# Attention on stacked high and low parts: two score products over 128 rows for three over 64, two value products for three

## The chip, the cores and the metric

One core of one Trainium2 chip runs the whole program. The metric is the device time of one execution in microseconds (us); lower is better. TensorE is called PE in the views, and its weight loads PEld; VectorE is DVE, ScalarE is ACT, GpSimd is POOL, and SyncE, which issues most of the DMAs, is SP.

## The reference, cut to what matters

The model has two layers on 1024 tokens of width 1024. Layer 0 is a gMLP mixer and an FFN; layer 1 is chunked band attention and an FFN. The change touches the attention only.

```python
def chunk_attention(h, w_qkv, rel_bias, w_out):      # SEQ 1024, 16 heads of 64, CHUNK 64
    ...
    def one_chunk(c):
        ...
        s = jnp.einsum('bqhd,bkhd->bhqk', qc, kc).astype(jnp.float32) * scale + bias
        ...
        p = jax.nn.softmax(s, axis=-1).astype(vc.dtype)
        return jnp.einsum('bhqk,bkhd->bqhd', p, vc)
    ...
    return o @ w_out
```

Each chunk of 64 queries sees its own chunk and the 8 chunks before it. Everything is float32.

## The kernel before, in words

**Split numbers.** TensorE multiplies in a shortened float32 (`F32R`). To keep the precision, each operand is held as a high part and a low part (the rest), and a product is three matmuls into one PSUM tile: high with high, high with low, low with high. The helper `product` issues them from lines 434, 435 and 436, so these three lines carry nearly all of TensorE's work, whatever the stage.

**Pairs of heads.** The attention walks over 8 pairs of heads. Pair 0 and pair 7 are written out, pairs 1 to 6 are one loop body. For each pair the projections q, k and v are made from the normed input (`part`, 8 products of 512 columns for each half of the tokens), and q of the next pair is made within this one. A pair of heads fills 128 partitions: head 0 is rows 0 to 63, head 1 rows 64 to 127.

**Steps and passes.** A pair has 16 steps s (8 blocks of 128 queries, two heads each). `step(s)` gives block i and head; the order of the blocks and heads is 0, 1 for head 0, then 0, 1 for head 1, then 2, 3, and so on. From step 8 on the window of keys is full, 640 columns (`WIN`); before that it is 128 to 512. The program has 19 passes m, in which the engines' work is laid out by hand as a pipeline:

- `scores_of(m)` on TensorE writes the scores into PSUM, DVE adds the bias and takes the row maximum (the custom instruction on L1142) and negates it (L1146), ACT takes the exponential (L856).
- For step m-1, DVE inverts the row sum (`rowinv`, L1128) and ACT scales the probabilities (L851).
- For step m-2, `transpose_probs` turns them on TensorE (L597) into `probs_t`, ACT copies the high part out (`pt_hi`, L846) and DVE makes the low part (`pt_lo`, L1132).
- In every second pass from 4 on, `values(c)` multiplies the turned probabilities of block pair c with `vz_hi` and `vz_lo` into bank 3. In `vz_*` the columns of the other head are zero, so that both heads add up in one 128-row tile of outputs: head 0 lands on partitions 0 to 63 and head 1 on 64 to 127.
- In passes 10 and 18, bank 3 holds the outputs of 512 queries; ACT copies the high part (`o_hi`, L867) and DVE the low part (`o_lo`, L1161), and `out_product` multiplies them with the output weights, one tile of 8 per slot (`out0` in passes 11 to 18, `out1p` in passes 3 to 7 of the next pair). DVE adds each to `x` (L1098).
- In pass 14, ACT and DVE take the next pair's q out of its bank (L825 and L1086).

Each engine runs its own instructions strictly in the written order, and the engines meet at semaphores. There is one `scores` tile and one `probs_t` tile: scores of pass m wait for the bias instruction of pass m-1, transposes of step s wait for the scaled probabilities of s and for `pt_lo` of s-1.

**Other engines.** POOL splits every weight unit into its two parts (L352, L354) from `raw`, which SP fills by DMA.

Of the kernel before, what the change touches and what calls it, by code (L numbers as in the profile page):

```python
# [82 lines left out]
def trunk(nc, x_t, gains, v_gain, w_s_t, b_s, rel_rev, ident_d, w_units, out_t):  # L83
# [4 lines left out]
    with ExitStack() as ctx:  # L88
# [65 lines left out]
        pt_lo += [sb("pt_lo1", [P, 2 * WIN // P, P], F32R)]  # L154
        o_hi = sb("o_hi", [P, HALF], F32R)
# [44 lines left out]
        bias_in, bias_masked, vz_zero = sem("bias_in"), sem("bias_masked"), sem("vz_zero")  # L200
# [98 lines left out]
        def in_heads(vz, h, view=lambda ap: ap):  # L299

            return view(vz[:, 4 * h:4 * h + 4, :, :]).rearrange("p t a (b c) -> p t (a b) c", c=HD)[:, :, 0::3, :]
# [128 lines left out]
        def _(pe):  # L430
# [147 lines left out]
            def scores_of(it, s):  # L578
                i, head = step(s)
                rows = slice(head * HD, (head + 1) * HD)  # L580
# [19 lines left out]
            def values(it, c):  # L600
# [5 lines left out]
                if c % 4 == 0:  # L606
                    ge(pe, o_lo_done, it * 2 + i // 4)

                both = [(key, 0, 2) for key in range(max(0, i - LEFT + 1), i + 1)]
                for key, q, n in both + ([(i - LEFT, 0, 1)] if i >= LEFT else []) + [(i + 1, 1, 1)]:  # L610
                    tiles = WIN // P
                    at = q * tiles + key - (i + q - LEFT)
                    cols = slice((i % 4 + q) * P, (i % 4 + q + n) * P)
                    out = bank[3][:, cols]
                    if n == 2:
# [82 lines left out]
        def _(act):  # L698
# [129 lines left out]
            def attention(it, first, last):  # L828
                def query_hi(it, h, name="q"):
                    p_hi_part(it, name, h, flipped(q_hi[:, toks(h)]), tiled(p_bank(it, name, h)[:, :]), HD ** -0.5)  # L830

                if first:
                    load_bias(0)
                    query_hi(-1, 0)
                    p_hi_part(it, "k", 0, k_hi[:, toks(0)])
                    hi_tiles(2, 1)
                    query_hi(0, 1, "q first")
                else:
                    p_hi_part(it, "k", 0, k_hi[:, toks(0)])
                p_hi_part(it, "k", 1, k_hi[:, toks(1)])  # L840
                for m in range(19):
# [17 lines left out]
                    if m in (1, 3):  # L859
                        p_hi_part(it, "vt", m // 2, in_heads(vz_hi, m // 2), by_head(p_bank(it, "vt", m // 2)))  # L860
# [43 lines left out]
        def _(dve):  # L904
# [179 lines left out]
            def query_lo(it, h, name="q", number=None):  # L1084
                dve.wait_ge(p_hi, it * 6 + (2 + 5 + h) if number is None else number)
                dve.scalar_tensor_tensor(flipped(q_lo[:, toks(h)]), tiled(p_bank(it, name, h)[:, :]), HD ** -0.5,  # L1086
                                         flipped(r32(q_hi[:, toks(h)])), ALU.mult, ALU.subtract).then_inc(p_read, 1)
# [7 lines left out]
            def attention(it, first, last):  # L1095
# [9 lines left out]
                def keys_lo(h, number):  # L1105
                    p_lo_part(it, "k", h, number, k_lo[:, toks(h)], r32(k_hi[:, toks(h)]))

                if first:
# [6 lines left out]
                    for part in (vz_hi, vz_lo):  # L1115
                        for head in range(2):
# [160 lines left out]
```

## Time and profile before

| what | us |
|---|---|
| median of 3 runs | 2829.72 |
| the three runs | 2825.27, 2831.75, 2829.72 |
| span of the profiled execution | 2829.8 |
| PE busy | 2715.2 (96%) |
| PEld busy | 2229.6 (79%) |
| DVE busy | 1244.1 (44%) |
| ACT busy | 594.2 (21%) |
| POOL busy | 798.9 (28%) |

The span runs from the first to the last instruction of one profiled execution; the page shows no time of its own around it, and the span lies 0.1 us from the median of the runs. The busy times are averages over stages that are limited by different things, so the attention is read by itself. It lies between about 1400 and 2074 us. A matmul's shown duration overlaps the next one's; what one costs in a dense row of them is the distance between their starts.

### The profile page before, as it was taken

What the parts mean: (1) busy time and instruction counts of PE and PEld (TensorE: products, weight loads), DVE (VectorE), ACT (ScalarE), POOL (GpSimd) and SP (SyncE); (2) the same over time, 40 slices, a digit from 0 to 9 for tenths busy, and PEclk for the clock granted to TensorE, in tenths of its full rate; (3) what the DMA queues carried; (4) which work ended last, traced back from release to release, by engine and by line L of the source; (5) the groups of instructions that cost most, each with busy time, mean ns of one, the idle gap of its engine ahead of it and who ended that gap; (6) DMA issues with size and microseconds to landing.
All of it is one profiled execution on the core that took longest, in us unless ns stands there. A gap on an engine that the chain in (4) does not pass through costs nothing.

```text
span 2829.8 us, 34050 instructions
## 1 busy us (share of the span) xinstructions
PE 2715.2 (96%) x12660; PEld 2229.6 (79%) x12660; DVE 1244.1 (44%) x1998; ACT 594.2 (21%) x1091; POOL 798.9 (28%) x450
## 2 busy tenths in 40 slices
PE   6999999998999999999899999999979999999997
PEld 5877877776888888888678888888758888888885
DVE  7215555567333322222754444455583233332225
ACT  3111111123000000000354433444430000000002
POOL 3232223223333333333211101111113333333334
PEclk9999999999999999999989999999999999999998
DMA  4222121111111111111100101110001111111101
GB/s 136 101 94 78 54 70 61 46 54 52 53 52 44 44 52 52 44 44 45 39 32 31 39 17 39 39 39 31 30 23 52 52 52 52 44 44 52 52 30 60
DMA packets 53220, 143.50 MB, mean 51 GB/s; under 512 B 5392, under 2 KB 15776, under 8 KB 53168
## 3 DMA queue, kind: packets, MB, share of 16 engines
q1 hardware_dynamic: 35632, 119.71, 12.8%
q10 hardware_dynamic: 17536, 23.07, 2.4%
q8 instruction: 35, 0.57, 0.1%
q14 instruction: 17, 0.14, 0.0%
HBM read 130.13 MB, written 12.63 MB: 50 GB/s over the span
## 4 chain that ended last, share of the span: by engine, by line
PE 45%; DVE 3%; issue 1%; ACT 1%; DVEq 0%; ACTq 0%
PE bank L434 11%; PE bank L436 10%; PE bank L435 10%; PE scores L434 3%; PE scores L435 2%; PE scores L436 2%; PE probs_t L597 2%; PE probs_t L436 1%; PE probs_t L435 1%; PE probs_t L434 1%; DVE full L927 0%; DVE prob L1142 0%; DVE rstd L917 0%; PE bank L648 0%; DVE acc L909 0%
## 5 line engine op out<-in xcount | busy, mean ns | idle before, releaser
L434 PE MATMUL bank<-hn_hi,w_hi 128*128 128x512 f32 x2048 | 818.3, 400 | 26.5 <-DVE hn_lo L932 22.1
L436 PE MATMUL bank<-hn_hi,w_lo 128*128 128x512 f32 x2048 | 805.3, 393 | 0.0
L435 PE MATMUL bank<-hn_lo,w_hi 128*128 128x512 f32 x2048 | 805.0, 393 | 0.0
L352 POOL TENSOR_SCALAR w_hi<-raw 128x1024 fp32r<-128x1024 f32 x212 | 248.1, 1170 | 1967.0 <-PE bank L436 1392.1
L354 POOL TENSOR_TENSOR w_lo<-raw,w_hi 128x1024 fp32r<-128x1024 f32 x212 | 518.2, 2444 | 17.7
L434 PEld LDWEIGHTS bank<-hn_hi,w_hi 128*128 128x128 f32 x2048 | 389.0, 190 | 119.1 <-DVE hn_lo L932 17.6
L436 PEld LDWEIGHTS bank<-hn_hi,w_lo 128*128 128x128 f32 x2048 | 389.0, 190 | 83.3
L435 PEld LDWEIGHTS bank<-hn_lo,w_hi 128*128 128x128 f32 x2048 | 389.5, 190 | 78.9 <-issue 1.2
L1002 DVE TENSOR_TENSOR full<-bank,atmp 128x512 f32<-128x512 f32 x88 | 60.9, 692 | 715.9 <-ACT atmp L806 714.3
L806 ACT ACTIVATE atmp<-bank 128x512 f32<-128x512 f32 x88 | 52.6, 598 | 1152.6 <-PE bank L436 1152.5
L1011 DVE TENSOR_TENSOR x<-probs_t,x 128x512 f32<-128x512 f32 x240 | 162.7, 686 | 110.6 <-PE probs_t L436 110.3
L1011 DVE TENSOR_TENSOR x<-scores,x 128x512 f32<-128x512 f32 x240 | 162.5, 687 | 95.6 <-PE scores L436 92.7
L1004 DVE TENSOR_TENSOR h_lo<-full,h_hi 128x512 fp32r<-128x512 f32 x88 | 128.5, 1460 | 61.5 <-ACT h_hi L767 61.5
L434 PE MATMUL scores<-h_hi,w_hi 128*128 128x512 f32 x352 | 137.5, 391 | 2.2 <-DVE h_lo L1004 1.6
L435 PE MATMUL scores<-h_lo,w_hi 128*128 128x512 f32 x352 | 137.3, 390 | 0.0
L436 PE MATMUL probs_t<-h_hi,w_lo 128*128 128x512 f32 x352 | 137.1, 390 | 0.0
L434 PE MATMUL probs_t<-h_hi,w_hi 128*128 128x512 f32 x352 | 136.9, 389 | 0.0
L435 PE MATMUL probs_t<-h_lo,w_hi 128*128 128x512 f32 x352 | 136.9, 389 | 0.0
L436 PE MATMUL scores<-h_hi,w_lo 128*128 128x512 f32 x352 | 136.9, 389 | 0.0
L856 ACT ACTIVATE prob<-prob,negmax 128x640 f32<-128x640 f32 (+4 forms) x128 | 89.2, 697 | 154.4 <-DVE negmax L1146 154.4
L1132 DVE TENSOR_TENSOR pt_lo<-probs_t,pt_hi 128x640 fp32r<-128x640 f32 (+4 forms) x128 | 83.7, 654 | 65.1 <-ACT pt_hi L846 63.6
L1098 DVE TENSOR_TENSOR x<-bank,x 128x512 f32<-128x512 f32 x128 | 86.1, 687 | 38.0 <-PE bank L436 37.2
(141 smaller groups left out, 3757.5 us busy)
## 6 DMA issues: line engine op xcount, KB each, us to landing
raw<-w_units_in SPq DMA_DIRECT2D x212, 512.0 KB, 3.3
v_raw<-v_scratch ACTq DMA_DIRECT2D x16, 512.0 KB, 4.4
bias<-rel_scratch ACTq DMA_DIRECT2D x8, 640.0 KB, 3.8
x<-x_t_in SPq DMA_DIRECT2D x16, 256.0 KB, 6.5
v_scratch<-atmp ACTq DMA_DIRECT2D x16, 256.0 KB, 2.5
v_scratch<-full ACTq DMA_DIRECT2D x16, 256.0 KB, 2.6
out_t<-x SPq DMA_DIRECT2D x16, 256.0 KB, 2.0
ws_raw<-w_s_t_in ACTq DMA_DIRECT2D x8, 64.0 KB, 4.0
```

What stands on the lines that cost most here:

```text
L352: pool.tensor_scalar(w_hi[slot][:, :], raw[r][:, :], 1.0, 1.0, ALU.mult, ALU.mult).then_inc(w_split, 1)
L354: pool.tensor_tensor(w_lo[slot][:, :], raw[r][:, :], r32(w_hi[slot][:, :]), ALU.subtract).then_inc(w_split, 1)
L434: pe.matmul(out, lh, rh, start=start, stop=False)
L435: pe.matmul(out, lh, rl, start=False, stop=False)
L436: last = pe.matmul(out, ll, rh, start=False, stop=stop)
L597: t = pe.transpose(probs_t[:, j * P:(j + 1) * P], prob[s % 2][:, j * P:(j + 1) * P], ident[:, :])
L856: act.activation(prob[m % 2][:, off:], prob[m % 2][:, off:], ACT.Exp, bias=negmax[:, m % 2:m % 2 + 1], accum_out=rowsum[:, m % 2:m % 2 + 1 ...
L1002: dve.tensor_tensor(full[f][:, :], up, in1, ALU.mult).then_inc(s.full, 1)
L1004: dve.tensor_tensor(lo[:, f, toks(h)], full[f][:, :], r32(hi_part[:, f, toks(h)]), ALU.subtract).then_inc(s.lo, 1)
L1011: dve.tensor_tensor(x[:, n, toks(h)], bank[4 + d % 4][:, :], x[:, n, toks(h)], ALU.add).then_inc(s.added, 1)
L1098: dve.tensor_tensor(x[:, n, toks(h)], p_bank(it, name, n)[:, :], x[:, n, toks(h)], ALU.add).then_inc(p_read, 1)
L1132: dve.tensor_tensor(pt_tiles(pt_lo, s), tiled(probs_t[:, window(s):WIN]), r32(pt_tiles(pt_hi, s)), ALU.subtract).then_inc(pt_lo_done, 1)
```

## The change

The query tile `q2` holds, for head 0, the high part on rows 0 to 63 and the low part on rows 64 to 127 (for head 1 the other way round). `k2_hi` holds the keys' high part on both halves of the rows, and `k2_lo` holds the low part on the head's own rows and zeros on the others. One matmul over 128 rows with `k2_hi` gives high-high plus low-high; one with `k2_lo` gives high-low. For the values, `v2` holds the high part in the head's own 64 columns and the low part in the other 64, in place of zeros. Two matmuls (with `pt_hi` and `pt_lo`) give the high parts' result on the head's own partitions and the low parts' result on the other 64. These two halves have to be added afterwards: each head has its own half of bank 3 now (256 queries at a time), ACT copies the side part across (`o_move`), and DVE adds it (`o_add`) into `o_full` in SBUF, from which `o_hi` and `o_lo` are made. The zeros of the `vz` tiles (4 memsets) go, those of `k2_lo` (2 memsets) come, and the first scores wait for them.

```diff
-        q_hi = sb("q_hi", [P, SEQ], F32R)
-        q_lo = sb("q_lo", [P, SEQ], F32R)
-        k_hi = sb("k_hi", [P, SEQ], F32R)
-        k_lo = sb("k_lo", [P, SEQ], F32R)
-        vz_hi = sb("vz_hi", [P, BLOCKS, 2, P], F32R)
-        vz_lo = sb("vz_lo", [P, BLOCKS, 2, P], F32R)
+        q2 = sb("q2", [P, 2, SEQ], F32R)
+        k2_hi = sb("k2_hi", [P, 2, SEQ], F32R)
+        k2_lo = sb("k2_lo", [P, 2, SEQ], F32R)
+        v2 = sb("v2", [P, BLOCKS, 2, P], F32R)
...
+        o_side = sb("o_side", [P, 2 * P])
+        o_full = sb("o_full", [P, HALF])
...
             def scores_of(it, s):
...
                 if s == 0:
                     pe.wait_ge(p_read, p_number(it, "k", 1) + 1)
+                    pe.wait_ge(k2_zero, 2)
...
-                    product(scores[:, SHIFT + at:SHIFT + to], (q_hi[rows, tq], q_lo[rows, tq]), (k_hi[rows, tk], k_lo[rows, tk]),
-                            True, True, qk_done if to == WIN else None)
+                    out = scores[:, SHIFT + at:SHIFT + to]
+                    pe.matmul(out, q2[:, head, tq], k2_hi[:, head, tk], start=True, stop=False)
+                    mm = pe.matmul(out, q2[:, head, tq], k2_lo[:, head, tk], start=False, stop=True)
+                mm.then_inc(qk_done, 1)
...
             def values(it, c):
...
-                if c % 4 == 0:
-                    ge(pe, o_lo_done, it * 2 + i // 4)
+                if c % 2 == 0:
+                    ge(pe, o_added, it * 8 + c)
...
-                    product(out, (vz_hi[:, key, head, :], vz_lo[:, key, head, :]), parts,
-                            head == 0 and key == both[0][0] and n == 2, head == 1 and q == 1,
-                            pv_done if q == 1 else None)
+                    pe.matmul(out, v2[:, key, head, :], parts[0], start=head == 0 and key == both[0][0] and n == 2, stop=False)
+                    mm = pe.matmul(out, v2[:, key, head, :], parts[1], start=False, stop=head == 1 and q == 1)
...
+                def key_hi(h):
+                    act.wait_ge(p_done, p_number(it, "k", h) + 1)
+                    for to in range(2):
+                        for head in range(2):
+                            op = act.activation(k2_hi[rows_of(head if to == 0 else 1 - head), head, toks(h)],
+                                                p_bank(it, "k", h)[rows_of(head), :], ACT.Copy)
+                    op.then_inc(p_hi, 1)
+
+                def o_move(tiles):
+                    act.wait_ge(pv_done, it * 8 + (2 * tiles + 2))
+                    ge(act, o_added, it * 8 + 2 * tiles)
+                    for head in range(2):
+                        act.activation(o_side[rows_of(head), :], bank[3][rows_of(1 - head), head * 2 * P:(head + 1) * 2 * P],
+                                       ACT.Copy).then_inc(o_moved, 1)
...
+                    if m in (6, 10, 14, 18):
+                        o_move((m - 6) // 4)
                     if m in (10, 18):
-                        act.wait_ge(pv_done, it * 8 + (4 if m == 10 else 8))
+                        act.wait_ge(o_added, it * 8 + (4 if m == 10 else 8))
...
-                        act.activation(flipped(o_hi[:, :]), tiled(bank[3][:, :]), ACT.Copy).then_inc(o_hi_done, 1)
+                        act.activation(flipped(o_hi[:, :]), tiled(o_full[:, :]), ACT.Copy).then_inc(o_hi_done, 1)
...
+                def o_add(tiles):
+                    ge(dve, o_hi_done, it * 2 + tiles // 2)
+                    dve.wait_ge(o_moved, it * 8 + (2 * tiles + 2))
+                    for head in range(2):
+                        rows = rows_of(head)
+                        dve.tensor_tensor(o_full[rows, tiles % 2 * 2 * P:(tiles % 2 + 1) * 2 * P],
+                                          bank[3][rows, head * 2 * P:(head + 1) * 2 * P], o_side[rows, :],
+                                          ALU.add).then_inc(o_added, 1)
...
                     if m == 14 and not last:
                         query_lo(it, 0)
...
+                    if m in (6, 10, 14, 18):
+                        o_add((m - 6) // 4)
```

The high part of q is now written in two instructions of 64 rows in place of one of 128, that of k in four; their low parts are made in two each. `key_hi` and `o_move` run on ACT, `o_add` on DVE.

How the instructions stand on ACT in pass 10 of a middle pair, before and then after the change; `o_side` is the tile that `o_move` fills, `pt_hi` the turned probabilities' high part:

```order
L856 ACTIVATE prob,rowsum<-prob,negmax 128x640
L864 REGISTER_ALU
L866 REGISTER_ALU
L867 ACTIVATE o_hi<-bank 128x4x128
L846 ACTIVATE pt_hi<-probs_t 128x640
```

```order
L885 ACTIVATE prob,rowsum<-prob,negmax 128x640
L855 REGISTER_ALU
L858 ACTIVATE o_side<-bank 64x256 x2
L897 REGISTER_ALU
L898 ACTIVATE o_hi<-o_full 128x4x128
L875 ACTIVATE pt_hi<-probs_t 128x640
```

Two copies stand ahead of `o_hi`, `o_hi` reads what DVE adds up in between, and the next step's `pt_hi` stands behind all of it.

The same for DVE in pass 14 of a middle pair, from the negated maximum of that pass to the low part of the next pass, before and then after:

```order
L1146 TENSOR_SCALAR negmax<-rowmax 128x1
L1085 REGISTER_ALU
L1086 SCALAR_TENSOR_TENSOR q_lo<-bank,q_hi 128x4x128
L1097 REGISTER_ALU
L1098 TENSOR_TENSOR x<-bank,x 128x512
L1128 RECIPROCAL rowinv<-rowsum 128x1
L1132 TENSOR_TENSOR pt_lo<-probs_t,pt_hi 128x640
```

```order
L1193 TENSOR_SCALAR negmax<-rowmax 128x1
L1116 REGISTER_ALU
L1118 SCALAR_TENSOR_TENSOR q<-bank,q 64x4x128 x2
L1149 REGISTER_ALU
L1152 TENSOR_TENSOR o_full<-bank,o_side 64x256 x2
L1131 REGISTER_ALU
L1132 TENSOR_TENSOR x<-bank,x 128x512
L1175 RECIPROCAL rowinv<-rowsum 128x1
L1179 TENSOR_TENSOR pt_lo<-probs_t,pt_hi 128x640
```

One instruction has become two, two more have come in between, and `rowinv` stands behind them.

## Rows read from the trace of the kernel before

**Rows 1.** The page's first line.

```profile
span 2829.8 us, 34050 instructions
```

**Rows 2.** Busy time by stretch, one pair of heads (start:end, us, busy us, clock, DMA).

```profile
1572.00:1654.00 82.00, 81.36 (x453) 67.32 (x452) 41.31 (x108) 35.41 (x73) 13.73 (x8) 1.00 0.10 34
```

**Rows 3.** PE's timeline, one pair: start, duration (us), line, operation.

```profile
1671.48 0.32 PE L434 MATMUL scores<-k_hi,q_hi 64*128 64x128 f32 x1
...
1700.92 0.71 PE L597 MATMUL probs_t<-ident,prob 128*128 128x128 f32 x5
1701.56 0.44 PE L434 MATMUL scores<-k_hi,q_hi 64*128 64x384 f32 x1
...
1702.19 0.28 PE L434 MATMUL scores<-k_hi,q_hi 64*128 64x256 f32 x1
1702.31 0.28 PE L435 MATMUL scores<-k_lo,q_hi 64*128 64x256 f32 x1
...
1702.63 0.39 PE L434 MATMUL bank<-pt_hi,vz_hi 128*128 128x256 f32 x1
...
1708.01 0.71 PE L597 MATMUL probs_t<-ident,prob 128*128 128x128 f32 x5
...
1721.80 0.71 PE L597 MATMUL probs_t<-ident,prob 128*128 128x128 f32 x5
...
1724.32 0.71 PE L597 MATMUL probs_t<-ident,prob 128*128 128x128 f32 x5
...
1728.32 0.71 PE L597 MATMUL probs_t<-ident,prob 128*128 128x128 f32 x5
```

**Rows 4.** Groups of instructions on PE in the attention, shapes apart.

```profile
L436 PE MATMUL bank<-pt_hi,vz_lo 128*128 128x256 f32 x192 | 54.4, 283 | 0.0
...
L436 PE MATMUL scores<-k_hi,q_lo 64*128 64x256 f32 x128 | 36.2, 283 | 0.0
...
L436 PE MATMUL scores<-k_hi,q_lo 64*128 64x384 f32 x64 | 21.5, 336 | 0.0
```

**Rows 5.** Timeline of ACT and DVE in pass 14 of the same pair.

```profile
1717.32 0.71 ACT L846 ACTIVATE pt_hi<-probs_t 128x640 fp32r<-128x640 f32 x1 [0.53 <-PE probs_t L597]
...
1718.06 0.83 DVE L1132 TENSOR_TENSOR pt_lo<-probs_t,pt_hi 128x640 fp32r<-128x640 f32 x1 [0.60 <-ACT pt_hi L846]
...
1718.80 0.81 DVE L1142 CUSTOM_DVE_ANT_0 prob<-scores,bias 128x640 f32<-128x640 f32 x1
...
1719.85 0.83 ACT L856 ACTIVATE prob<-prob,negmax 128x640 f32<-128x640 f32 x1 [1.11 <-DVE negmax L1146]
...
1720.67 0.57 ACT L825 ACTIVATE q_hi<-bank 128x512 fp32r<-128x512 f32 x1
...
1721.28 0.69 DVE L1086 SCALAR_TENSOR_TENSOR q_lo<-bank,q_hi 128x512 fp32r<-128x512 f32 x1 [1.47 <-ACT q_hi L825]
...
1722.61 0.15 DVE L1128 RECIPROCAL rowinv<-rowsum 128x1 f32<-128x1 f32 x1
```

**Rows 6.** Timeline in pass 10: the outputs' high and low parts.

```profile
1705.09 0.58 ACT L867 ACTIVATE o_hi<-bank 128x512 fp32r<-128x512 f32 x1
...
1705.70 0.69 DVE L1161 TENSOR_TENSOR o_lo<-bank,o_hi 128x512 fp32r<-128x512 f32 x1 [1.47 <-ACT o_hi L867]
```

**Rows 7.** Timeline: instructions of 256 columns on ACT and DVE.

```profile
1686.60 0.36 ACT L846 ACTIVATE pt_hi<-probs_t 128x256 fp32r<-128x256 f32 x1
...
1686.99 0.42 DVE L1132 TENSOR_TENSOR pt_lo<-probs_t,pt_hi 128x256 fp32r<-128x256 f32 x1
```

**Rows 8.** Timeline at the start of pair 0, PE and then DVE.

```profile
1421.99 0.32 PE L434 MATMUL scores<-k_hi,q_hi 64*128 64x128 f32 x1 [1.41 <-DVE k_lo L1082]
...
1421.99 1.02 DVE L1117 MEMSET vz_hi<- 128x512 f32 x2
```

**Rows 9.** Busy time by stretch behind pair 7: PE first, the granted clock third from the end.

```profile
2066.58:2069.99 3.41, 0.00 (x0) 0.00 (x0) 3.37 (x4) 0.34 (x1) 0.00 (x0) 1.00 0.00 0
2069.99:2073.41 3.42, 3.14 (x7) 2.29 (x8) 3.42 (x7) 0.96 (x3) 0.00 (x0) 0.50 0.00 0
```

More of the change, by code:

```diff
@@ L297, in tiled, with rows_of, v2_part @@
             return ap.rearrange("p (t c) -> p t c", c=P)
-        def in_heads(vz, h, view=lambda ap: ap):
-            return view(vz[:, 4 * h:4 * h + 4, :, :]).rearrange("p t a (b c) -> p t (a b) c", c=HD)[:, :, 0::3, :]
+        def rows_of(head):
+            return slice(head * HD, (head + 1) * HD)
+        def v2_part(h, lo):
+            quarters = v2[:, 4 * h:4 * h + 4, :, :].rearrange("p t a (b c) -> p t (a b) c", c=HD)
+            return quarters[:, :, 1:3, :] if lo else quarters[:, :, 0::3, :]
         def by_head(ap):
@@ L829, in query_hi @@
                 def query_hi(it, h, name="q"):
-                    p_hi_part(it, name, h, flipped(q_hi[:, toks(h)]), tiled(p_bank(it, name, h)[:, :]), HD ** -0.5)
+                    act.wait_ge(p_done, p_number(it, name, h) + 1)
+                    for head in range(2):
+                        op = act.activation(flipped(q2[rows_of(head), head, toks(h)]),
+                                            tiled(p_bank(it, name, h)[rows_of(head), :]), ACT.Copy, scale=HD ** -0.5)
+                    op.then_inc(p_hi, 1)
[5 more added lines that the diff above has]
+                                                p_bank(it, "k", h)[rows_of(head), :], ACT.Copy)
+                    op.then_inc(p_hi, 1)
+                def o_move(tiles):
[4 more added lines that the diff above has]
+                                       ACT.Copy).then_inc(o_moved, 1)
                 if first:
@@ L838, in attention @@
                 else:
[L839 to L840 removed]
+                    key_hi(0)
+                key_hi(1)
                 for m in range(19):
@@ L1085, in query_lo @@
                 dve.wait_ge(p_hi, it * 6 + (2 + 5 + h) if number is None else number)
-                dve.scalar_tensor_tensor(flipped(q_lo[:, toks(h)]), tiled(p_bank(it, name, h)[:, :]), HD ** -0.5,
-                                         flipped(r32(q_hi[:, toks(h)])), ALU.mult, ALU.subtract).then_inc(p_read, 1)
+                for head in range(2):
+                    op = dve.scalar_tensor_tensor(flipped(q2[rows_of(1 - head), head, toks(h)]),
+                                                  tiled(p_bank(it, name, h)[rows_of(head), :]), HD ** -0.5,
+                                                  flipped(r32(q2[rows_of(head), head, toks(h)])), ALU.mult, ALU.subtract)
+                op.then_inc(p_read, 1)
             def mask_bias(it):
@@ L1105, in keys_lo @@
                 def keys_lo(h, number):
-                    p_lo_part(it, "k", h, number, k_lo[:, toks(h)], r32(k_hi[:, toks(h)]))
+                    dve.wait_ge(p_hi, it * 6 + (2 + number))
+                    for head in range(2):
+                        rows = rows_of(head)
+                        op = dve.tensor_tensor(k2_lo[rows, head, toks(h)], p_bank(it, "k", h)[rows, :],
+                                               r32(k2_hi[rows, head, toks(h)]), ALU.subtract)
+                    op.then_inc(p_read, 1)
+                def o_add(tiles):
+                    ge(dve, o_hi_done, it * 2 + tiles // 2)
+                    dve.wait_ge(o_moved, it * 8 + (2 * tiles + 2))
+                    for head in range(2):
+                        rows = rows_of(head)
+                        dve.tensor_tensor(o_full[rows, tiles % 2 * 2 * P:(tiles % 2 + 1) * 2 * P],
+                                          bank[3][rows, head * 2 * P:(head + 1) * 2 * P], o_side[rows, :],
+                                          ALU.add).then_inc(o_added, 1)
                 if first:
@@ L1114, in attention @@
                     keys_lo(1, 2)
-                    for part in (vz_hi, vz_lo):
-                        for head in range(2):
-                            dve.memset(r32(part[:, :, head, (1 - head) * HD:(2 - head) * HD]), 0.0).then_inc(vz_zero, 1)
+                    for head in range(2):
+                        dve.memset(r32(k2_lo[rows_of(1 - head), head, :]), 0.0).then_inc(k2_zero, 1)
                     mask_bias(0)
@@ L1158, in attention @@
                         out_add("out1p", 1, n)
+                    if m in (6, 10, 14, 18):
+                        o_add((m - 6) // 4)
                     if m in (10, 18):
                         dve.wait_ge(o_hi_done, it * 2 + (1 if m == 10 else 2))
-                        dve.tensor_tensor(flipped(o_lo[:, :]), tiled(bank[3][:, :]), flipped(r32(o_hi[:, :])),
+                        dve.tensor_tensor(flipped(o_lo[:, :]), tiled(o_full[:, :]), flipped(r32(o_hi[:, :])),
                                           ALU.subtract).then_inc(o_lo_done, 1)
```

16 lines of the change are left out of this document (9 added, 7 removed).

## The prediction

> **What bounds the kernel now.** The page gives the span [rows 1]; nothing is shown around it, and it lies 0.1 us above the median of the runs, so I sum against 2829.8. The change lives in the attention only, so the next view is the busy time of one pair of heads: in 82 us TensorE (PE) is busy for 81.4, VectorE (DVE) for 41.3 and ScalarE (ACT) for 35.4 [rows 2]. That reads like a pair bound by TensorE, from which every matmul taken away is time won. The timelines are read next, to see how far behind TensorE the softmax loop of ACT and DVE is, since a busy share can't show that. The reader should see a loop with a period of its own, little below what TensorE takes.
>
> **What TensorE saves.** A matmul costs the distance to the next start. A third product over 256 columns costs 0.12 us (1702.31 after 1702.19) [rows 3]. Over 384 columns it is 0.17: the three of that size run from 1701.56 to 1702.19, 0.63 us, of which I put down 0.11 to the first, below. Over 128 columns I take 0.11 (five transposes of 128 columns and what follows them take 0.64) [rows 3]. The scores have 64, 128 and 32 groups of 384, 256 and 128 columns, the values 192 of 256 and 96 of 128 ([rows 4]; the 128-column ones are counted from the code). Per pair that is 8 x 0.17 + 16 x 0.12 + 4 x 0.11 = 3.7 us and 24 x 0.12 + 12 x 0.11 = 4.2 us. The switch to products over 64 rows costs too. From the transposes at 1700.92 to the first values product at 1702.63 is 1.71 us; five transposes (0.55) and six products (0.87) explain 1.42. The other 0.29, and another 0.11 on the first product behind (0.39 in place of 0.28), are the change between 128 rows and 64 [rows 3]. 128-row products behind transposes keep some 0.08 of it. So 0.32 a step, 16 steps, 5.1 us a pair. All in all TensorE has 13.0 us a pair less to do, 104 us over 8 pairs; without the switch it is 7.9 and 63. The Trainium skill, "TensorEngine Tiling (Array Packing)", Key Properties, says that changing the tiling mode drains the engine; by it the switch goes away in full, as in the larger sum.
>
> **What sets the pace instead.** Take pass 14 [rows 5]. `pt_hi` starts at 1717.32, `pt_lo` at 1718.06, the bias and maximum at 1718.80, the exponential at 1719.85, and the next instruction on ACT at 1720.67; in pass 13 that next one is again `pt_hi`. Its period is 0.74 + 0.74 + 1.05 + 0.82 = 3.35 us for a full step, whatever TensorE does. Any instruction put between these on ACT or DVE lengthens it.
>
> I walk through a pair, with time 0 at its first scores product (1671.48). Before, the transposes start at 29.4 (step 8), 36.5 (step 10), 50.3 (13), 52.8 (14) and 56.8 (15) [rows 3].
>
> **Passes 0 to 9.** TensorE saves 6.1 us: the ten score steps 5.2, the values 0.9. The early steps wait at several places for `norm`, the v copies and the x adds, which don't get faster; and in pass 6 `o_move` and `o_add` are new. Two ACT copies of 64x256 are priced by the nearest row, 128x256 at 0.36 us [rows 7], as 0.7; two DVE adds by 0.42 [rows 7] as 0.75; both may be 0.5 at the least or 1.2 (two of 512 columns, [rows 6]) at the most. DVE's add stands ahead of `rowinv`, which delays the step by about 0.9. I take 2.4 of the 6.1 as kept: step 8 turns at 27.0. Bounds: 1.4 and 4.0.
>
> **Passes 10 and 11.** The exponential of pass 10 ends at 32.1. Before, `o_hi` (0.5 to the next instruction) followed and then `pt_hi`. Now: two copies to 32.8, two adds to 33.5, `o_hi` to 34.1, `o_lo` to 34.8 (0.61 to its end for the next; [rows 6]). ACT stands still in between, because `o_hi` waits for DVE. Behind it stand `pt_hi` of step 9 (34.0 in place of 32.6) and everything of step 10. TensorE waits for `o_lo` from 33.0 to 34.9 with its first `out0` product. Step 10 turns at 35.9, 0.6 earlier than before: 1.8 of the 2.4 is given back.
>
> **Steps 10 to 13.** The loop needs 3 x 3.35 = 10.1 us, TensorE 13.8 less three score steps (1.8) and two of values (1.4): 10.6. TensorE is the later one here, and the gain is kept: step 13 turns at 46.5, 3.8 earlier.
>
> **Pass 14.** Here ACT has `o_move` and both q instructions, DVE both low parts of q, `o_add` and an x add, all before `rowinv` of step 14. Before: from the exponential's start (1719.85) to `rowinv` (1722.61) 2.76 us [rows 5]. Now the exponential starts at 46.7: ACT free 47.6, copies to 48.2, two q instructions of 64 rows to 49.3 (0.5 each, assuming that half the rows take as long as all; no row shows it, bound 0.3), two low parts to 50.6 (0.61 each), two adds to 51.2, x add to 51.8, `rowinv`; then the scaling (0.2 + 0.82) to 52.9. Step 14 turns at 52.9, where it turned at 52.8 before. TensorE has run out of work at 48.4 and waits for 4.5 us: the 3.8 us are all gone. By the lower bounds it would be 51.6.
>
> **The rest.** From step 14 to 15 TensorE is the later one again: 4.0 - 0.7 = 3.3, step 15 at 56.2, 0.6 earlier, and the last values save 0.7. The longer q and k copies (four instructions of 0.5 and two of 0.6 for a half of the keys, 2.1 more) lie beside 16 us of dense projections. A middle pair is 1.3 us shorter, of 13.0 hoped for; six of them 7.8.
>
> **Pair 0 and pair 7.** In pair 0 TensorE already waits for `k_lo`, 1.41 us [rows 8]. There are now three more copies and one more low part ahead of it, and about 2 us of zeros (two of 64x1024, each the price of two memsets at 0.5, [rows 8]) stand before the first scores, no longer behind them. That makes the first scores some 5 us later; the waits that pair 0 has anyway take part of it up, and I put it at +2.4. Pair 7 has no dense projections for the next pair, runs at the loop's pace already, and gets `o_move` and `o_add`: +1.8. Sum without more: 2829.8 - 7.8 + 2.4 + 1.8 = 2826.
>
> **The clock.** Behind pair 7, TensorE does nothing for 3.4 us at granted clock 1.00 (2.4 GHz), and then runs 3.4 us at 0.50 (1.2 GHz) although it is busy for 3.1 of them [rows 9]. The new wait in pass 14 is 4.5 us and comes in seven pairs. What follows it (transposes, q, values) is bound by TensorE, so each microsecond at the lower level loses half. One such stretch loses 1.7, two lose 3.4; I take 2.2, in 85% of the pairs, 1.9 a pair, 13 us in seven. The forecast is 2826 + 13 = 2839. The Trainium skill, "TensorE: Matmul & The Clock Gate", HAM oscillation, describes such a loop: a wait between bursts that drops the clock each time, so that each burst starts slow.
>
> **The rivals.** (1) *The same walk with no clock drop*: 2826, no change to be measured. For it: the first wait of a pair that is long enough is mine, not measured; it shrinks if the half-row instructions are shorter than I assume, and the row shows a drop behind a wait of its own length alone. (2) *Shorter half-row instructions and a kept gain*: at 51.6 in pass 14 and 1 us more kept in pass 10, a pair gains 3.6; over 8 pairs, less the ends, 2800 to 2820. (3) *The loop doesn't bind*: TensorE's whole 63 to 104 us arrive, 2726 to 2767. Against it speaks the loop of 3.35 us, read from start times. (4) *The clock stays low for longer*, through the 8 us of work from step 14 to the projections: then 4 to 8 us a pair, 2826 + 7 x 7 = 2875. What decides between faster and slower is whether the clock drops behind the wait in pass 14: one slow stretch costs 1.7 us, and a middle pair has gained 1.3.
>
> **How the numbers follow.** Clock drop, likeliest: 0.50, of itself 2832 to 2850. Rival 1: 0.20. Rival 2: 0.14. Rival 3: 0.05. Rival 4: 0.11. A measurement of this kernel tells 0.2% (5.7 us) from no change. Slower: 0.46 of the first and all of the fourth, less a little for a walk that is too pessimistic, 0.55. Same: 0.26. Faster: 0.19. The range from 2812 to 2862 leaves out rival 3, part of rivals 2 and 4.
>
> **What the profile would show.** If right: products over 128 rows with no gap around the scores; the same number of us per pair within 2; TensorE idle in pass 11 for `o_lo` and longest in front of the transposes of step 14, released by ACT's scaling; and granted clock 0.50 once in a pair, behind that wait. Wrong if the wait in pass 14 is under 2 us, if the clock stays at 1.00 in the pairs, or if half-row instructions take clearly other than full-row ones.

## The result and the profile after

| what | before | after |
|---|---|---|
| median of 4 runs, us | 2830.73 | 2862.87 |
| lowest and highest run | 2825.27, 2835.54 | 2861.58, 2864.01 |
| ratio of the medians, 95% interval | | 1.0106, 1.0086 to 1.0126 |

The change makes the kernel slower by 32 us, where 9 were forecast. The direction is the forecast's, the size is not. As a time the median lies 0.9 us above the range; the kernel before had 2829.72 when the range was set and 2830.73 here, and as a change the 32.1 us lie 0.1 inside it. A run takes 1.9 us more than its span (2861.58 against 2859.7; before 2831.75 against 2829.8), the same in both, so spans can be compared. The page's first lines:

```profile
span 2859.7 us, 33352 instructions
PE 2649.0 (93%) x12148; PEld 2178.8 (76%) x12148; DVE 1302.1 (46%) x2092; ACT 656.4 (23%) x1219; POOL 801.3 (28%) x450
```

TensorE is busy for 66 us less than before, and the span is 30 us longer [rows 1]. So the question is what TensorE now waits for. Its waits in the attention (who waits, for whom, us in total, times, longest one):

```profile
PE probs_t L605 <- ACT prob L880: 44.3, 33, 5.0
PE probs_t L605 <- DVE pt_lo L1179: 22.7, 25, 2.1
PE bank L440 <- DVE o_lo L1210: 15.4, 7, 2.5
PE bank L440 <- DVE hn_lo L963: 7.9, 1, 7.9
...
PE scores L596 <- DVE k_lo L1164: 6.8, 1, 6.8
```

The transposes wait for the softmax for 67 us. Before, the same view has 2.0 us for them, in four waits. One middle pair by the busy time of its engines (start:end, length, then PE, PEld, DVE, ACT and POOL busy; the granted clock stands third from the end):

```profile
1684.85:1770.10 85.25, 74.06 (x389) 61.86 (x388) 48.31 (x120) 43.20 (x88) 14.01 (x8) 0.94 0.09 32
```

The pair begins with its first scores product and ends just before that of the next one, which starts at 1770.17. It has TensorE busy for 74 us, where it was 81 [rows 2], and is still 3.2 us longer than the 82.1 of before. The same pair on TensorE's timeline, to be read against [rows 3]:

```profile
1684.85 0.22 PE L596 MATMUL scores<-k_hi,q 128*128 128x128 f32 x1
...
1712.38 0.74 PE L605 MATMUL probs_t<-ident,prob 128*128 128x128 f32 x5 [0.21 <-DVE pt_lo L1179]
...
1715.71 0.74 PE L605 MATMUL probs_t<-ident,prob 128*128 128x128 f32 x5 [0.94 <-DVE pt_lo L1179]
...
1720.76 0.58 PE L440 MATMUL bank<-o_hi,w_hi 128*128 128x512 f32 x1 [2.15 <-DVE o_lo L1210]
...
1721.99 1.27 PE L605 MATMUL probs_t<-ident,prob 128*128 128x128 f32 x5
...
1733.52 0.71 PE L605 MATMUL probs_t<-ident,prob 128*128 128x128 f32 x5
...
1739.94 1.33 PE L605 MATMUL probs_t<-ident,prob 128*128 128x128 f32 x5 [4.43 <-ACT prob L880]
...
1745.62 0.71 PE L605 MATMUL probs_t<-ident,prob 128*128 128x128 f32 x5
```

The waits stand in brackets: 2.15 us for `o_lo` in pass 11 and 4.43 us for the scaled probabilities in front of step 14. Behind each, five transposes take 1.3 us in place of 0.7. That is the clock, as the same stretches by busy time show:

```profile
1717.60:1721.00 3.40, 1.25 (x6) 0.73 (x5) 1.87 (x5) 2.12 (x5) 0.00 (x0) 1.00 0.35 130
1721.00:1724.40 3.40, 3.40 (x14) 2.97 (x14) 2.59 (x7) 2.44 (x5) 0.00 (x0) 0.50 0.00 0
...
1734.70:1738.10 3.40, 0.81 (x4) 0.32 (x3) 2.09 (x4) 1.89 (x3) 0.00 (x0) 1.00 0.00 0
1738.10:1741.50 3.40, 1.56 (x7) 1.47 (x8) 3.14 (x8) 1.62 (x3) 0.00 (x0) 0.50 0.00 0
1741.50:1744.90 3.40, 3.40 (x16) 3.21 (x14) 0.99 (x2) 1.43 (x4) 0.00 (x0) 0.50 0.57 193
```

The granted clock falls from 1.00 (2.4 GHz) to 0.50 (1.2 GHz) twice in the pair, once for 3.4 us and once for 6.8, each time behind a stretch in which TensorE was busy for 1.25 or 0.81 of 3.4 us. The second low stretch begins in the wait, 1.8 us before step 14 turns (1738.10 against 1739.94). Over the whole execution the clock is at 0.50 for 168 us, before for 100. Five of the six middle pairs have both low stretches and take 85.3 us. The first of them has only the one at step 14, although its wait for `o_lo` is 2.17 us, and takes 84.8:

```profile
1514.71:1599.53 84.82, 73.08 (x390) 60.50 (x389) 48.30 (x120) 43.11 (x88) 14.07 (x8) 0.96 0.10 33
```

What comes ahead of the two waits is ACT's and DVE's work in passes 10 and 14, to be read against [rows 6] and [rows 5]:

```profile
1717.47 0.78 ACT L858 ACTIVATE o_side<-bank 64x256 f32<-64x256 f32 x2
...
1719.28 0.63 ACT L898 ACTIVATE o_hi<-o_full 128x512 fp32r<-128x512 f32 x1 [1.02 <-DVE o_full L1152]
...
1733.90 0.78 ACT L858 ACTIVATE o_side<-bank 64x256 f32<-64x256 f32 x2
1734.71 1.20 ACT L841 ACTIVATE q<-bank 64x512 fp32r<-64x512 f32 x2
...
1739.06 0.83 ACT L880 ACTIVATE prob<-prob,rowinv 128x640 f32<-128x640 f32 x1 [2.43 <-DVE rowinv L1175]
```

```profile
1718.29 0.88 DVE L1152 TENSOR_TENSOR o_full<-bank,o_side 64x256 f32<-64x256 f32 x2 [1.80 <-ACT o_side L858]
1719.94 0.69 DVE L1210 TENSOR_TENSOR o_lo<-o_full,o_hi 128x512 fp32r<-128x512 f32 x1 [0.77 <-ACT o_hi L898]
...
1735.93 1.39 DVE L1118 SCALAR_TENSOR_TENSOR q<-bank,q 64x512 fp32r<-64x512 f32 x2 [3.02 <-ACT q L841]
1737.36 0.88 DVE L1152 TENSOR_TENSOR o_full<-bank,o_side 64x256 f32<-64x256 f32 x2
1738.27 0.69 DVE L1132 TENSOR_TENSOR x<-bank,x 128x512 f32<-128x512 f32 x1
1738.87 0.15 DVE L1175 RECIPROCAL rowinv<-rowsum 128x1 f32<-128x1 f32 x1
```

In pass 14 one engine after the other stands still: DVE 3.02 us for ACT's q copies, then ACT 2.43 us for `rowinv`, and TensorE 4.43 us for ACT. Two copies of 64 rows take as long as two of 128 would (0.60 us each for 512 columns, where one of 128 rows is shown with 0.57 in [rows 5]).

**Where the 29.9 us are.** Both kernels' executions were cut at the first scores products of the pairs. Pair 0 begins at 1428.97 in place of 1421.99: +7.0. Pair 0 itself takes 85.74 in place of 85.23: +0.5. The six middle pairs take 511.45 (1514.71 to 2026.16) in place of 492.79: +18.7, 3.1 each on average. Pair 7, up to its last output product, takes 78.38 in place of 74.55: +3.8. That makes 30.0.

### The profile page after: what moved, and what is told of

Read it like the earlier page. It is cut to its first block, busy times and chain, and to the rows that moved or that the text cites. A ratio compares the mean times of both kernels' runs of the same rounds, so it can differ in the third digit from the quotient of the medians.

```text
span 2859.7 us, 33352 instructions
## 1 busy us (share of the span) xinstructions
PE 2649.0 (93%) x12148; PEld 2178.8 (76%) x12148; DVE 1302.1 (46%) x2092; ACT 656.4 (23%) x1219; POOL 801.3 (28%) x450
## 4 chain that ended last, share of the span: by engine, by line
PE 77%; DVE 12%; issue 5%; ACT 4%; DMA 0%; DVEq 0%; ACTq 0%; SPq 0%
PE bank L440 17%; PE bank L442 16%; PE bank L441 16%; PE scores L440 4%; PE scores L441 4%; PE scores L442 4%; PE probs_t L442 4%; PE probs_t L440 4%; PE probs_t L441 4%; DVE prob L1189 2%; DVE full L958 2%; DVE v_lo L1065 1%; DVE acc L940 1%; ACT pt_hi L875 1%; DVE x L1132 1%
## 5 line engine op out<-in xcount | busy, mean ns | idle before, releaser
L605 PE MATMUL probs_t<-ident,prob 128*128 128x128 f32 x480 | 85.0, 302 | 67.2 <-ACT prob L880 44.3
L605 PEld LDWEIGHTS probs_t<-ident,prob 128*128 128x128 f32 x480 | 60.8, 153 | 96.5 <-ACT prob L880 90.2
```

The lines of the kernel that those rows point to most:

```text
L605: t = pe.transpose(probs_t[:, j * P:(j + 1) * P], prob[s % 2][:, j * P:(j + 1) * P], ident[:, :])
```

## The experiments

**Theory A** is the forecast's mechanism with the sizes read above: the loop of ACT and DVE sets the pace, the work that the change puts into it in passes 10 and 14 uses up what TensorE saves, and the clock drops at the two waits take the rest. **The rivals** lay the loss elsewhere: on the start (the zeros of `k2_lo` ahead of the first scores), on one half of the change alone, whatever the other does, or on the instructions themselves with no part for the clock. The texts of the expectations name what each would give.

The first four ran together; the kernel before had 2832.61 beside them.

**One half at a time.** `s_only` takes the stacked scores and leaves the values as before (three products, `vz_hi`, `vz_lo`, no side path; to fit, it has a smaller scratch area for DMA descriptors). `v_only` takes the stacked values and leaves the scores.

```diff
 s_only, against after
-                    pe.matmul(out, v2[:, key, head, :], parts[0], start=..., stop=False)
-                    mm = pe.matmul(out, v2[:, key, head, :], parts[1], start=False, stop=...)
+                    product(out, (vz_hi[:, key, head, :], vz_lo[:, key, head, :]), parts, ...)
-                    if m in (6, 10, 14, 18):
-                        o_move((m - 6) // 4)
...
-                    if m in (6, 10, 14, 18):
-                        o_add((m - 6) // 4)
 v_only, against after
-                    pe.matmul(out, q2[:, head, tq], k2_hi[:, head, tk], start=True, stop=False)
-                    mm = pe.matmul(out, q2[:, head, tq], k2_lo[:, head, tk], start=False, stop=True)
+                    product(scores[:, SHIFT + at:SHIFT + to], (q_hi[rows, tq], q_lo[rows, tq]), (k_hi[rows, tk], k_lo[rows, tk]), ...)
```

> The scores part of the change alone: two products over 128 rows, with the doubled key copies and the zeros, and the values as before (three products, no side copy and add). Theory A (the side copies and adds in passes 6, 10 and 14 lengthen the softmax loop, and the waits that they make drop the clock): about 2815 us, since 8.8 us of TensorE work a pair go, some 3 us of it are kept under the loop, pair 0 starts about 6 us later, and the clock stays at 1.00 in the middle pairs. Theory B (the doubled and halved copies of q and k are what costs): 2845 us or more. Theory C (TensorE alone sets the pace): 2760 us.

> The values part of the change alone: two products, side copy and add in passes 6, 10, 14 and 18, scores as before over 64 rows. Theory A: slower than before, 2840 to 2855 us, with TensorE waiting in pass 11 and in front of step 14, and perhaps a low clock behind it in each pair. Theory B (the q and k copies cost): 2800 us, since 4.2 us a pair of TensorE work go. If A holds, its loss and the gain or loss of the scores part add up to more than the whole change's, since the waits share the same places.

Measured: `s_only` 2811.85, ratio 0.9922 (0.9905 to 0.9939), faster. `v_only` 2842.99, ratio 1.0040 (1.0025 to 1.0056), slower. Against the before beside them (2832.61) they are 21 us less and 10 more, 10 less in sum; the whole change is 32 us more. So the halves are not independent, which fits two halves that use the same slack. The text of `v_only` expected a departure from the sum with the other sign, the halves costing more than the whole. A pair of `s_only`, its wait in front of step 14, and its waits for the softmax in all pairs:

```profile
1669.90:1748.50 78.60, 74.29 (x426) 62.54 (x425) 44.05 (x112) 39.65 (x80) 13.73 (x8) 1.00 0.10 35
...
1719.17 0.77 PE L601 MATMUL probs_t<-ident,prob 128*128 128x128 f32 x5 [1.99 <-ACT prob L867]
...
PE probs_t L601 <- ACT prob L867: 20.6, 25, 2.0
```

Without the side path, and with the values' third products back, the wait is 1.99 us in place of 4.43, and the granted clock stays at 1.00 for the whole pair. `v_only` happens to show the price of the clock inside one execution (the profiled one is one of two that took 2851 us; the other three took 2841 to 2843). Its six middle pairs take 82.68, 85.75, 85.70, 84.25, 85.76 and 82.67 us, with the same instructions in each. Two of them:

```profile
1506.62:1589.30 82.68, 78.47 (x418) 63.05 (x417) 45.41 (x116) 38.49 (x80) 14.08 (x8) 1.00 0.10 34
1675.05:1760.75 85.70, 81.44 (x417) 65.61 (x417) 45.38 (x116) 38.61 (x80) 14.07 (x8) 0.96 0.09 32
```

The ones of 82.7 have the clock at 1.00 throughout; in those of 85.7 it is at 0.50 for 6.8 us, and in that of 84.25 for 3.4. TensorE's longest waits in these six pairs are short (window 1506 to 2013):

```profile
PE probs_t L604 <- ACT prob L867: 10.8, 12, 1.6
PE bank L441 <- DVE o_lo L1187: 9.4, 6, 1.6
```

The same work, with the same waits of at most 1.6 us, comes with a drop in one pair and not in another, and a low stretch of 6.8 us costs 3.0, one of 3.4 us 1.6.

**The waits kept, TensorE busy in them.** Before the first and the fifth `out0` product, TensorE runs matmuls whose results are overwritten, in the time in which it would wait.

```diff
+BUSY = {0: 8, 4: 14}
...
+                if name == "out0" and n in BUSY:
+                    for _ in range(BUSY[n]):
+                        pe.matmul(out[:, :], k2_hi[:, 0, 0:P], k2_hi[:, 0, 0:512], start=True, stop=True)
+                    if n == 0:
+                        pe.wait_ge(o_lo_done, it * 2 + 1)
```

> The changed kernel with idle TensorE time filled by products whose result is overwritten: 8 of 512 columns before the first output product of pass 11 and 14 before that of pass 15, each into the bank that the product then overwrites. They take 1.8 and 3.2 us of waits of 2.2 and 4.4 us. Theory A (clock): the granted clock stays at 1.00 in the pairs, what follows the waits runs at full speed, 3.0 to 3.5 us a pair less, 2835 to 2842 us. Rival (the length of the chain is all there is): 2863 us or more, since work is only added.

Measured: 2843.52, ratio 1.0035 (1.0021 to 1.0049). The kernel has 22 more matmuls in a pair and is 19 us faster than the one without them, 1.5 us above what theory A expected. The busy times of a pair, and TensorE's rows at the extra matmuls:

```profile
1681.84:1764.41 82.57, 75.85 (x412) 62.48 (x411) 48.29 (x120) 43.11 (x88) 14.06 (x8) 1.00 0.10 33
...
1730.64 3.35 PE L583 MATMUL bank<-k_hi 128*128 128x512 f32 x14
...
1736.50 0.76 PE L611 MATMUL probs_t<-ident,prob 128*128 128x128 f32 x5 [1.82 <-ACT prob L885]
```

The clock is at 1.00 over the whole pair, in all six middle pairs, and the pair is 2.7 us shorter than that of after. Adding work can't shorten the chain of waits, so these 2.7 us a pair, 16 of the 19 us, are shown to be the clock's. 82.57 is still 0.4 above the pair of before: with the clock at 1.00, and the extra matmuls in it, the change gains nothing in a middle pair. Of the 18.7 us that the six middle pairs lose, the clock thus has 16 and the chain 2.7.

**The side path taken out.** `no_side` is after without `o_move` and `o_add`; bank 3 is laid out as before, and `o_hi` and `o_lo` are read from it. It leaves out the half of the values' result that comes from the low parts of v.

```diff
-                    if m in (6, 10, 14, 18):
-                        o_move((m - 6) // 4)
-                        act.wait_ge(o_added, it * 8 + (4 if m == 10 else 8))
+                        act.wait_ge(pv_done, it * 8 + (4 if m == 10 else 8))
-                        act.activation(flipped(o_hi[:, :]), tiled(o_full[:, :]), ACT.Copy).then_inc(o_hi_done, 1)
+                        act.activation(flipped(o_hi[:, :]), tiled(bank[3][:, :]), ACT.Copy).then_inc(o_hi_done, 1)
```

> The changed kernel without the side copies and adds: the low parts' half of the result is left out, bank 3 is laid out and read as before. Everything else of the change is there, and TensorE has as little to do as in the change. Theory A: the softmax loop of 3.35 us for a full step is what is left, no low clock in the middle pairs, 2800 to 2815 us. Rival (TensorE would set the pace without the side path): 2740 to 2760 us.

Measured: 2808.88, ratio 0.9917 (0.9901 to 0.9934). Four copies and four adds of 0.4 us in each half of a pair are worth 54 us in all, with what they bring on. Yet `no_side` has both stackings, and is only 3 us below `s_only`, which has one, with intervals that overlap: of the 4.2 us a pair, 34 in all, that two products for three save at the values next to nothing arrives.

```profile
1664.65:1743.38 78.73, 72.15 (x390) 59.84 (x388) 43.94 (x112) 39.64 (x80) 13.70 (x8) 0.98 0.10 35
```

Its pair is as long as that of `s_only` (78.6), with 36 fewer matmuls and TensorE idle for 6.6 us of it; a low stretch of the clock of 3.4 us explains 1.7 at most. Theory A had expected no low clock in the middle pairs; all six have this one, at step 14, where the wait is 3.15 us. The rest of the idle time is not the clock's: something else sets this length.

**The loop, shortened.** If it is the softmax loop, a shorter DVE instruction in it should move the time in the new kernel and hardly in the old. `pt_lo` is made for 16 of each 128 columns only; the others are zeros, set once (so a part of the probabilities' low parts is left out).

```diff
+                    for part in pt_lo:
+                        dve.memset(r32(part[:, :, :]), 0.0)
...
-                        dve.tensor_tensor(pt_tiles(pt_lo, s), tiled(probs_t[:, window(s):WIN]),
-                                          r32(pt_tiles(pt_hi, s)), ALU.subtract).then_inc(pt_lo_done, 1)
+                        dve.tensor_tensor(pt_tiles(pt_lo, s)[:, :, 0:16], tiled(probs_t[:, window(s):WIN])[:, :, 0:16],
+                                          r32(pt_tiles(pt_hi, s))[:, :, 0:16], ALU.subtract).then_inc(pt_lo_done, 1)
```

> The kernel before with a shorter softmax loop: VectorE's low part of the turned probabilities is made for 16 of each 128 columns only (the others stay zero), which leaves out part of the values' low product and takes some 0.5 us from each full step of the loop, 3.35 to about 2.85 us. TensorE's work is the same. If TensorE sets the pace before the change: little gain, 2812 to 2828 us, from the early passes and pair 7 alone. If the loop sets it already: 16 steps x 0.4 x 8, 50 us less, 2780 us.

> The same edit on the changed kernel without the side copies and adds (which leaves out the low parts' half of the result, and here seven eighths of the low part of the probabilities too). Theory A (under the change the loop and no longer TensorE sets the pace): the shorter loop tells here, 25 to 45 us below the version with the full loop (2808.9), 2765 to 2785 us. Rival (something else than the loop holds it, such as the weight split on GpSimd or the dense projections): 2795 us or more.

Measured beside a before of 2832.13, both as theory A expected: on the kernel before 2824.85, ratio 0.9974 (0.9964 to 0.9983), 7 us; on `no_side` 2773.67, ratio 0.9794 (0.9776 to 0.9812), 35 us below `no_side`. One and the same edit is worth five times as much in the new kernel. A pair of the first, and then one of the second:

```profile
1671.13:1753.19 82.06, 81.42 (x453) 67.66 (x452) 35.09 (x108) 35.57 (x72) 13.72 (x8) 1.00 0.10 34
```

```profile
1728.20:1803.74 75.54, 71.01 (x390) 59.72 (x388) 37.82 (x112) 39.94 (x80) 13.76 (x8) 0.98 0.11 36
```

The old pair stays at 82.1, since TensorE is busy in all of it; the new one falls from 78.7 to 75.5, with a low stretch of 3.4 us in either. This shows that the bound has changed hands, for the change without its side path; the edit was not run on the whole change, whose loop is longer still. Of the six middle pairs of the short `no_side`, four have that low stretch, at a wait of 2.13 us, and two have the same wait and none:

```profile
1578.68:1652.67 73.99, 69.42 (x389) 58.27 (x388) 37.81 (x112) 39.85 (x80) 13.76 (x8) 1.00 0.11 37
```

**The zeros moved.** The two memsets of `k2_lo` go ahead of pair 0's second low parts of q and k on DVE, where it waits for ACT; once in after, once in `s_only`.

```diff
                     tiles(2, 1)
+                    for head in range(2):
+                        dve.memset(r32(k2_lo[rows_of(1 - head), head, :]), 0.0).then_inc(k2_zero, 1)
                     query_lo(0, 1, "q first", 3)
                     keys_lo(1, 2)
-                    for head in range(2):
-                        dve.memset(r32(k2_lo[rows_of(1 - head), head, :]), 0.0).then_inc(k2_zero, 1)
```

> The whole change with the zeros moved in the same way. 2 us less than the changed kernel, 2859 to 2862 us, if the zeros are on the path; no difference if the key copies alone are. The low clock of pair 0 may take another place, which is worth up to 5 us either way.

> The scores part alone, with the two memsets of the zeros in k2_lo moved ahead of the low part of the first q on VectorE, where it waits 3.8 us for ScalarE anyway. In the scores part alone TensorE waited 6.8 us there, in the kernel before 1.4. Theory (the zeros stand on the path to the first scores): about 2 us less than the scores part alone, 2808 to 2811 us, and the wait 4.8 us. Rival (the longer wait comes from the key copies alone): no difference, and the wait stays at 6.8.

Measured beside a before of 2833.49: 2860.68, ratio 1.0091 (1.0075 to 1.0108), and 2808.87, ratio 0.9905 (0.9888 to 0.9921). The intervals overlap those of after and of `s_only`. The wait itself, first in `s_only` and then with the zeros moved:

```profile
PE scores L592 <- DVE k_lo L1140: 6.8, 1, 6.8
```

```profile
PE scores L592 <- DVE k_lo L1128: 4.5, 1, 4.5
```

So the zeros are worth 2.3 us of this wait, in after as in `s_only` (6.8 and 4.46 us there). In `s_only` that arrives: pair 1 begins 3.1 us earlier (1509.74 in place of 1512.84). In the whole change it does not: the first scores come 1.5 us earlier, but pair 1 begins at 1514.72, where it began at 1514.71, because pair 0 takes 1.5 us more, with 27 us of low clock in place of 22. No gain of `zeros_early` is therefore shown. `s_zeros` has the shortest time of the kernels that compute everything, 25 us below before.

**The side path a pass later.** If what hurts is that the copies and adds meet the q instructions in pass 14, they should cost less in pass 15; `late_busy` adds the extra matmuls to it.

```diff
-                    if m in (6, 10, 14, 18):
+                    if m in (7, 10, 15, 18):
                         o_move((m - 6) // 4)
...
+BUSY = {0: 8, 4: 6}     (late_busy alone)
```

> The whole change with the side copy and add of the first and the third quarter one pass later (passes 7 and 15 in place of 6 and 14), so that pass 14 has only the q instructions of its own. Theory A (what stands ahead of the row sum's inverse in pass 14 makes the 4.4 us wait, and the wait drops the clock): the wait in front of step 14 falls to about 2.8 us, the low clock behind it is shorter or gone, 2 to 4 us a pair, 2835 to 2850 us. Rival (the side path costs the same wherever it stands): 2860 to 2865 us, with the wait one step later.

> The same with idle time filled by products whose result is overwritten: 8 ahead of the first output product in pass 11, 6 ahead of that in pass 15. If the late side path shortens the chain by itself, this is 5 to 12 us below the kernel with busy waits alone (2843.5), 2832 to 2838 us; if the late version only gains by the clock, the two are the same, 2841 to 2846 us.

Measured: 2865.55, ratio 1.0115 (1.0098 to 1.0132), and 2861.88, ratio 1.0096 (1.0080 to 1.0113). Theory A expected a gain of 10 us and more for `late` and was wrong; for `late_busy` both figures of the text (2832 to 2838, and 2841 to 2846 for a gain by the clock alone) were missed by 15 us and more. The rival's figure for `late` is met within 1 us. The waits of `late`:

```profile
PE probs_t L605 <- ACT prob L880: 27.4, 31, 3.2
PE bank L627 <- DVE o_full L1152: 21.7, 15, 2.9
PE bank L440 <- DVE o_lo L1210: 15.4, 7, 2.5
PE probs_t L605 <- DVE pt_lo L1179: 13.5, 19, 1.6
```

The transposes wait 26 us less (27.4 and 13.5 in place of 44.3 and 22.7), and 21.7 us come up on a line that had none: the values of the next two blocks start a new sum in bank 3, and have to wait until DVE has added up the old one. The wait has moved, not gone. In all six middle pairs the clock still drops, for 3.4 and 6.8 us in `late` and for 6.8 in `late_busy`, although the wait in front of step 14 is down to 2.59 and 1.77 us. A pair of `late_busy` there:

```profile
1741.60 0.77 PE L611 MATMUL probs_t<-ident,prob 128*128 128x128 f32 x5 [1.77 <-ACT prob L885]
...
1745.05 0.58 PE L633 MATMUL bank<-pt_hi,v 128*128 128x256 f32 x1 [1.99 <-DVE o_full L1157]
```

```profile
1743.20:1746.60 3.40, 1.55 (x7) 1.55 (x8) 2.33 (x5) 2.32 (x5) 0.00 (x0) 0.50 0.50 193
```

`busy_waits` had a wait of 1.82 us at this place and 10 us of work behind it, and kept the clock. Here a second wait, the one for `o_full`, follows 1.5 us after the first, and the clock is down from about its start. That the two waits together do it is the reading that fits; a run with more than 6 extra matmuls, or with some in the second wait, would have to show it. Nor did the first stretch, which the 8 extra matmuls took away, shorten the pair: it is 85.4 us with one low stretch as with two.

## Why the prediction was right and wrong

**What bounds, and what TensorE saves: right.** From the transposes of step 12 to the next dense products, 1.71 us and 0.11 more on the first product became 1.13 with 0.01, in a pass with scores and no values. That is 0.68 us less where the terms of the forecast (third products 0.29, switch 0.32) give 0.61. The Trainium skill, "TensorEngine Tiling (Array Packing)", Key Properties, has the drain at a change of mode; by what went away with the 64-row products, the trace agrees, with some 0.4 us for both directions together. And the savings were not worth their sum, as forecast: `no_side` shows the products at the values to be worth next to nothing, and the two `short` kernels show why. Of the signs that the prediction named, TensorE's two waits came where they were forecast, and no sign of being wrong came true. Two signs of being right did not: the pair was to keep its length within 2 us and is 3.2 longer, and the clock was to be low once in a pair and is so twice.

**The walk through a pair: right in its order, too short in its sizes.** From the first scores product, forecast and measured:

| transposes of step | 8 | 10 | 13 | 14 | 15 | next pair |
|---|---|---|---|---|---|---|
| forecast, clock apart | 27.0 | 35.9 | 46.5 | 52.9 | 56.2 | 80.8 |
| after | 27.5 | 37.1 | 48.7 | 55.1 | 60.8 | 85.3 |
| `busy_waits`, clock 1.00 | 27.5 | 36.9 | 47.7 | 54.7 | 58.0 | 82.6 |

The last row is the one to hold against the forecast: 0.5 us late by step 8 (of "I take 2.4 of the 6.1 as kept", 1.9 was kept), 0.5 more in pass 10, 0.2 up to step 13, 0.6 in pass 14, and then nothing. The first `out0` product was put at 34.9 and came at 35.9: beside the 0.5 us brought along, the copies and adds took 0.78 and 0.88 in place of 0.7 and 0.7, and the four handovers between ACT, DVE and TensorE 0.03 to 0.13 us each, 0.3 in all, where the sum had 0.1. Pass 14 is the same: from the exponential's start to the transposes 7.0 us in place of 6.2, with q copies of 0.60 and adds of 0.44. The chain in that pass and its members were forecast rightly; "half the rows take as long as all" holds. That the wait itself met its figure so closely (4.43 us against 4.5) is partly luck: the slow stretch in pass 11 had made TensorE 1.0 us late for it, and in the middle pair without that stretch the wait is 5.0 us. In all, a middle pair without the clock is 0.4 us longer than before, not 1.3 shorter: 1.7 us a pair, 10 us in six.

**The clock: right in kind, too small.** "I take 2.2, in 85% of the pairs", one stretch behind pass 14. There are two stretches in five of the six middle pairs, the one at step 14 in all six, and from `busy_waits` to after a pair loses 2.7 us. By the table, 0.4 of it is there at step 14 and 2.4 more at step 15. So the second stretch had nearly its forecast size (2.2), but comes in every pair; the first, in pass 11, was not in the sum at all, costs 1.0 us up to step 13, and gives all but 0.4 back in the wait that follows. The pair without it is 0.5 us shorter. The wait for `o_lo` that comes with it was forecast at 1.9 us (33.0 to 34.9) and is 2.15, but was given no drop; the row of before showed one behind 3.4 us [rows 9]. The Trainium skill, "TensorE: Matmul & The Clock Gate", HAM oscillation, has the loop of wait and slow burst; the trace agrees, with a slow stretch at the wait of step 14 in every middle pair. Together the miss is 0.8 us a pair, 5 us in six.

**The ends: too small.** For pair 0, "+2.4" was a start 5 us late of which waits would take a part. The start is 7.0 us late, because the longer q and k instructions of the first half of the tokens (ACT 3.6 us for what took 1.2) also stand ahead of `hn_lo`, for which TensorE waits 7.92 us in place of 6.15; that was not in the sum. Then 5.4 us more on `k_lo`. The pair itself is only 0.5 longer where a middle one is 3.1. Its own waits may have taken up part of the difference, but its clock was low in the old kernel too (17 us of it, now 22), so how much they took is not shown. With the clock this is +7.5 in place of +4.3. Pair 7: +3.8 in place of +1.8, a figure that had no clock in it, with 10 us of low clock in place of 3.4.

The four misses are 10, 5, 3 and 2 us, 20 of the 21 that lie between +9.2 in the sum of the forecast and +29.9 of the profiled executions. None of them changes the mechanism, and all have one sign. The largest, and part of the start's, is work on a path priced from rows in which that work was not on the path, with the handovers hidden; the second is a low stretch that the sum did not have, and the last two hold some of either, unseparated.

**The rivals.** Rival 3 (the loop does not bind) is refuted by the `short` kernels. Rival 2 is refuted by 0.59 to 0.60 us for copies of 64 rows. Rival 1 needs the clock to stay up; `busy_waits` has that in the middle pairs and is at 2843.5, not 2826. Rival 4 (clock low through the whole rest, 4 to 8 us a pair) came nearest in time (2875) and was wrong in its size: the low stretch at step 14 ended after 6.8 us, 1.8 of them still in the wait, and cost 2.4 us, not 4 to 8. Its nearness in time is luck, from misses elsewhere.

## What to carry to other kernels

When an engine looks saturated, look first at how far behind it the next loop is: here TensorE had 13 us a pair to give by the forecast's sum, and the loop of the other two engines let 3.5 through where no side path stood in it. Price work that is put on that loop by its handovers too, and ask of two halves of a change whether they draw on the same slack: stacked scores alone were worth 21 us, stacked values alone cost 10, both together cost 32. And count every wait on TensorE of some 2 us, not just the longest, as one at which the clock may drop: of the kernels here with one such wait or two in a middle pair, `s_only` (2.0 us) never lost the clock, `v_only` (1.6 us, twice) and the short `no_side` (2.1 us) lost it in four pairs of six.

## What was not expected of the hardware

- The granted clock fell to 0.50 at a wait of 2.15 to 2.17 us in five of the six middle pairs of after and stayed at 1.00 at one of 2.17 us in the first of them; in `v_only`, whose waits there were at most 1.6 us, it fell in four of six pairs with the same instructions.
- 22 matmuls whose results are not needed, set into the waits of a pair, make the kernel 19 us faster.
- On ACT and DVE, instructions on 64 rows take what those on 128 take: 0.60 and 0.69 us for 512 columns, 0.39 and 0.44 for 256.
